# Twelve of the twenty modulation vectors of a two-block transformer kernel are finished one step later in the order of the engines

## The reference, cut to what matters

```python
c_act  = silu(c);  cc_act = silu(c_ctx)
mod_l = (c_act @ ada_w[i] + ada_b[i])[:, None, :]      # ada_w[i]: 1024 x 6144
mod_c = cc_act @ ada_w[i] + ada_b[i]
sh_a, sc_a, g_a, sh_m, sc_m, g_m = split(mod_l, 6)
h_l = modulate(rms_norm(x, norm_mix_g[i]), sh_a, sc_a)
...
x = x + g_a * y_l
x = x + g_m * mlp(modulate(rms_norm(x, norm_mlp_g[i]), sh_m, sc_m))
```

## Time and profile before

| what | value |
|---|---|
| time, median of 3 runs | 2417.89 us (2416.68 to 2421.29) |
| profiled execution, its own time | 2426.14 us |
| profiled execution, span of its instructions | 2424.2 us |
| granted TensorE clock, mean | 0.994 |
| TensorE busy with matmuls | 2386.3 us, 98% of the span |
| VectorE busy | 1610.2 us, 66% |
| ScalarE busy | 1192.7 us, 49% |
| GpSimd busy | 331.6 us, 14% |

### The profile page before, as it was taken

The page is one execution under the profiler, slowest core; times in us unless marked ns, Lnnn a source line. Parts: engine busy times, 40 slices in busy tenths (PEclk is TensorE's granted clock), DMA queues, the critical chain, the costliest instruction groups (busy, mean ns, idle before and its releaser), DMA issues.

```text
span 2424.2 us, 40267 instructions
## 1 busy us (share of the span) xinstructions
PE 2386.3 (98%) x17001; PEld 2189.1 (90%) x17001; DVE 1610.2 (66%) x2428; ACT 1192.7 (49%) x1977; POOL 331.6 (14%) x362
## 2 busy tenths in 40 slices
PE   8999999999999999999999999999999999999998
PEld 7999889999999998999997758878889888889998
DVE  5676676887777677678866865765653655466753
ACT  5445665544444567655554642421333444455643
POOL 1311002232132100035330001000001000001000
PEclk9999999999999999999999989999999999999999
DMA  7768634676676783466763211345542433334552
GB/s 238 228 224 221 201 109 135 219 237 208 217 241 224 208 224 121 123 200 223 244 200 108 55 46 53 122 166 182 189 158 87 150 104 105 120 117 146 179 195 96
DMA packets 374113, 401.54 MB, mean 166 GB/s; under 512 B 44708, under 2 KB 346048, under 8 KB 373677
## 3 DMA queue, kind: packets, MB, share of 16 engines
q1 hardware_dynamic: 371160, 391.19, 51.3%
q10 hardware_dynamic: 2772, 7.78, 1.0%
HBM read 397.87 MB, written 4.22 MB: 166 GB/s over the span
## 4 chain that ended last, share of the span: by engine, by line
PE 82%; DVE 11%; ACT 3%; issue 1%; POOL 1%; SPq 1%; DMA 0%; DVEq 0%; ACTq 0%; POOLq 0%
PE bank L685 25%; PE bank L687 24%; PE bank L686 24%; DVE rounded L2479 4%; PE bank L693 3%; DVE plain L2454 2%; ACT rounded L1670 2%; PE bank L698 1%; PE bank L1109 1%; PE bank L1139 1%; DVE plain L2464 0%; DVE plain L2712 0%; DVE plain L2752 0%; PE bank L1310 0%; ACT plain L2073 0%
## 5 line engine op out<-in xcount | busy, mean ns | idle before, releaser
L685 PE MATMUL bank<-rounded 128*128 128x256 f32 (+2 forms) x3480 | 1079.5, 310 | 7.5 <-DVE rounded L2479 2.9
L686 PE MATMUL bank<-rounded 128*128 128x256 f32 (+2 forms) x3480 | 1065.3, 306 | 0.0
L687 PE MATMUL bank<-rounded 128*128 128x256 f32 (+2 forms) x3480 | 1065.2, 306 | 0.0
L2479 DVE TENSOR_TENSOR rounded<-plain,rounded 128x1024 fp32r<-128x1024 f32 (+1 forms) x630 | 737.0, 1217 | 409.1 <-ACT rounded L1670 408.9
L1670 ACT ACTIVATE rounded<-plain 128x1024 fp32r<-128x1024 f32 (+1 forms) x630 | 616.4, 1032 | 359.1 <-PE bank L687 267.7
L685 PEld LDWEIGHTS bank<-rounded 128*128 128x128 f32 x3480 | 665.3, 191 | 53.5 <-issue 9.6
L687 PEld LDWEIGHTS bank<-rounded 128*128 128x128 f32 x3480 | 665.4, 191 | 29.0
L686 PEld LDWEIGHTS bank<-rounded 128*128 128x128 f32 x3480 | 665.7, 191 | 28.0
L685 PE MATMUL bank<-rounded,rounded 128*128 128x256 f32 (+2 forms) x1472 | 449.0, 305 | 5.7 <-DVE rounded L2479 2.3
L687 PE MATMUL bank<-rounded,rounded 128*128 128x256 f32 (+2 forms) x1472 | 445.4, 303 | 0.0
L686 PE MATMUL bank<-rounded,rounded 128*128 128x256 f32 (+2 forms) x1472 | 445.4, 303 | 0.0
(11 more groups left out here) (313 smaller groups left out, 1861.1 us busy)
## 6 DMA issues: line engine op xcount, KB each, us to landing
plain<-in_mlp_w SPq DMA_DIRECT2D x64, 1024.0 KB, 5.3
plain<-in_ada_w SPq DMA_DIRECT2D x48, 1024.0 KB, 5.5
plain<-in_ffn_w_gate SPq DMA_DIRECT2D x44, 1024.0 KB, 5.7
plain<-in_ffn_w_up SPq DMA_DIRECT2D x44, 1024.0 KB, 5.5
plain<-in_ffn_w_down SPq DMA_DIRECT2D x32, 1024.0 KB, 5.6
plain<-in_w_in SPq DMA_DIRECT2D x32, 1024.0 KB, 5.4
plain<-in_od_w_in SPq DMA_DIRECT2D x32, 1024.0 KB, 5.4
plain<-in_ffn_w_down SPq DMA_DIRECT2D x16, 768.0 KB, 6.3
```

The costliest lines, as they stand in the source:

```text
L685: pe.matmul(dst, a[0], b[0], start=first and i == 0, stop=False)
L686: pe.matmul(dst, a[0], b[1], start=False, stop=False)
L687: ins = pe.matmul(dst, a[1], b[0], start=False, stop=last and i == n - 1)
L2479: dve.tensor_tensor(low, raw, top, SUB).then_inc(*done(("lo", m, half)))
```

## The change

The step of vector 0 of each piece becomes the one after the step of its fourth `ada_w` unit. Vector 1 stays where it was: `step + 1 + 1` is the old `step + 2`, and `step + 1 + 2` the old `step + 3`. So 12 of the 20 vectors move by one step, and 8 don't.

```diff
@@ -103,7 +103,7 @@
     for (s, step), u in ADA_AT.items():
         if u % 4 == 3:
             for v in CHUNKS[u // 4][2]:
-                out[s, step + (3 if step == 26 else 2) * v] = (u // 4, v)
+                out[s, step + 1 + (2 if step == 26 else 1) * v] = (u // 4, v)
     return out
```

## The result

| | kernel before | changed kernel |
|---|---|---|
| median | 2419.05 us (22 runs, 2416.68 to 2424.94) | 2424.3 us (22 runs, 2418.34 to 2429.04 but for one) |
| ratio | | 1.0018, 95% interval 1.0011 to 1.0024 |
| profiled execution: its time, span | 2426.14, 2424.2 us | 2420.28, 2418.4 us |

The changed kernel is slower by some 4.4 us (2.7 to 5.8 by the interval). I had forecast 1.6 us and a time of 2419.5 us, at most 2423.0. One run of the changed kernel, at a mean clock of 0.751 and 2877.21 us, is left out of the ratio. The trace of the changed kernel is at the same time 5.8 us *shorter* than that of the kernel before. So a single pair of traces can't be subtracted as a whole; it has to be read place by place.

A forecast was written before the change was run, and what follows sets the result against it. TensorE, busy 98% of the span, was taken to bound the kernel. Twelve places paying 0.27 us less six saving it made 1.6 us, VectorE, banks and transfers 0: 2417.89 + 1.6 = 2419.5 us, range 2416.0 to 2423.0 us.

The forecast's parts named there:

- What bounds the kernel, and the two kinds of place: TensorE, busy 98%, bounds; at six of twelve old places it waits for VectorE's low half (4.52 us together), at six not.
- The term of the sum: On TensorE, twelve new places each pay 0.27 us and six old ones without a wait save it: 1.6 us longer.
- The larger sum that the prediction also gives and turns down: Starts of line 799's eight matmuls at least 25 ns apart: 0.11 us more per place, 2.3 us in all.
- VectorE, banks, transfers at nothing: Moved bias additions on VectorE, the ring of banks, fold buffers and `ada_w` transfers delay nothing: cost 0.
- step 12 of p0, where I expected a wait of some tenths: VectorE's line 2611 waits a few tenths of a microsecond for its products, only at this place; cost 0.
- The range and the chances: Whole kernel: 2416.0 to 2423.0 us; chances 0.05 slower by over 0.2%, 0.02 faster, 0.93 within 0.2%.
- rival 3: At step 5 of p0, idle time grown to 1.65 us halves the clock: 1.7 or 6.8 us more; chance 0.05.

The follow-up runs named there:

- e8: The changed kernel with the two folds of each piece put behind VectorE's next low halves instead of ahead of them; ratio to the kernel before 0.9992 (0.9983 to 1.0001).
- e2: Half of the change: against the kernel before, only the seven vectors of stages a0, b0, a1 and b1 move; ratio 1.0004 (0.9993 to 1.0015), median 2422.27 us.
- e3: The other half of the change: against the kernel before, only the five vectors of p0 move; ratio 1.0001 (0.9988 to 1.0014).
- e6: The kernel before with one vector alone moved, that of a1 at step 26; ratio 1.0002 (0.9994 to 1.0011).
- e1: The changed kernel once more, unaltered, against the kernel before; ratio 1.0017 (1.0004 to 1.0029), median 2425.03 us.
- e4: The kernel before with nothing moved, but three unread products (about 1.35 us) added as a delay at step 29 of a0; ratio 1.0008 (0.9998 to 1.0019).
- e5: Control: the kernel before, word for word, against itself; ratio 1.0006 (0.9998 to 1.0015).
- e7: The kernel before with vector 1 put at the old step of vector 0 instead of two or three steps later; ratio 1.0002 (0.9993 to 1.0010).
- e9: The kernel before with seven unread products keeping TensorE busy ahead of two waits of the convolution stage; ratio 0.9988 (0.9979 to 0.9997).
- e10: The changed kernel with seven unread products keeping TensorE busy ahead of two waits of the convolution stage; mean 2419.02 us (12 runs).
- e11: The changed kernel with both the later folds of e8 and the unread products of e10; median 2412.40 us, ratio to the kernel before 0.9964 (0.9950 to 0.9978).

## Why the prediction was wrong

**What bounds the kernel, and the two kinds of place:** right. Six of the twelve places had a wait in front, VectorE's row of multiply-adds and folds ahead of the low halves is what it is for (e8 takes it away and the waits go), and the waits grew by 0.18 us without the products.

**The term of the sum:** right in kind, and mis-sized: this is the first step that failed. "I take 0.27 us for each" stopped at the first matmul behind the products. The second is late by a further 0.10 us with 256 columns. By the lags of e2 and e3 a place costs 0.37 us five times and 0.41 us once: 5 x 0.37 + 0.41 = 2.3 us in place of 6 x 0.27 = 1.6 us. The row for it (the second matmul behind the products) is the one behind the last that I had read. The larger sum that the prediction also gives and turns down is 2.3 us as well, but by luck: it puts the missing time between the starts of the eight small matmuls, and these still lie within 0.06 us of each other (0.25 us for all, 0.19 for one).

**VectorE, banks, transfers at nothing:** right where it can be seen. Line 2611 has no idle time before it at any of the twenty places in the first trace of the change. At b0 it starts at 525.77 us, 4.5 us behind its products. At step 12 of p0, where I expected a wait of some tenths, it starts at 1654.57 us directly behind two low halves:

```profile
1652.29 2.36 DVE L2479 TENSOR_TENSOR rounded<-plain,rounded 128x1024 fp32r<-128x1024 f32 x2 [1.58 <-ACT rounded L1670]
1654.57 0.16 DVE L2611 TENSOR_TENSOR plain<-bank,plain 128x8 f32<-128x8 f32 x1
1659.80 0.88 DVE L2560 SCALAR_TENSOR_TENSOR plain<-bank,plain 128x256 f32<-128x256 f32 x2 [5.07 <-PE bank L687]
```

It arrives 0.7 us behind the products of 1653.84 us, and the idle time falls to the wait of line 2560 behind it, as reasoned.

**The range and the chances:** the second step that failed, and the larger one. I set them from the three runs shown, "its three runs lie 4.6 us apart", and took the rest of the kernel as fixed. It isn't: 93 later runs of the kernel before reach from 2416.36 to 2428.2 us, and the lower the mean clock of a run, the longer it is (correlation -0.80). The sign of it was on the table: the profiled execution was 8.3 us above the median. The reason stands in the earlier trace rows, and I used them for rival 3, which put the fall of the clock at step 5 of p0. There the wait of 1.65 us left the clock at 1.00 in every trace, as the work ahead of it had let me expect; the falls are where they were before, but for one at 797 us in e6.

**What is left.** Fixed cost 2.3 us, measured 4.35 (2.7 to 5.8) and in e1 4.1 us (1.0 to 7.0). The record can part the two, since it has the mean granted clock of every run. A stretch at half clock loses half of its length, so a run of 2420 us has lost about 2420 x (1 - mean clock) in all. This is an estimate: not all of that time is work that would have gone twice as fast (the 3.4 us of e6 cost 1.5 us and not 1.7), and the clock is on record in steps of 0.001, or 2.4 us. Here is the mean of each kernel against the kernel before beside it, as timed, then with this loss taken off every run, and by the lag of its one trace (without the shift at 260 us). Behind each is half of the 95% interval, from the spread of the runs:

| run | as timed, us | without the clock, us | by the lag, us |
|---|---|---|---|
| e1 | +3.6, 2.5 | +2.8, 1.5 | +2.6 |
| e2 | +1.1, 1.8 | +2.9, 1.3 | +2.2 |
| e3 | +0.5, 2.4 | +1.1, 1.6 | +0.4 |
| e4 | +1.4, 2.0 | +0.4, 1.2 | +1.0 |
| e5 (before) | +1.1, 1.7 | -1.2, 1.7 | +0.1 |
| e7 | 0.0, 1.9 | -3.3, 1.1 | -2.5 |
| e8 | -1.2, 1.8 | -4.6, 1.1 | -4.1 |
| e9 | -3.5, 1.8 | +0.5, 1.2 | -0.3 |
| e10 | -1.9, 1.6 | +2.5, 1.4 | +2.2 |
| e11 | -8.9, 1.4 | -4.4, 1.8 | -4.0 |

In all ten rows the difference without the clock agrees, within its interval, with what the lag says, and the gain of e9 is nothing but clock. In e6, which is not in the table, it does not agree (-0.9, 1.8 against 2.7 us by the lag), but the lag of its one trace holds the late transfer and 1.5 us of low clock. The 33 runs of the changed kernel are 2.6 us (1.8 to 3.3) above the 93 of before when the clock is taken off, and 2.8 us if 0.001 of clock is put at 1.8 us, as a straight line through the 93 runs has it. So outside the clock no more is seen than the fixed cost, with what the wait at 797 us may add.

The clock itself: the mean is 0.9952 in the 33 runs and 0.9956 in the 93, which makes 0.8 us, with 1.3 us to either side. That the change lowers it is not shown. The kernel before, set against itself in e5, has 0.9950 beside 0.9959, and e4 has 0.9949, no higher than the 0.9954 and 0.9950 of the two sets of runs of the changed kernel. In the first comparison part of the difference may also lie with the other side: its 22 runs of the kernel before have a mean of 2419.4 us, the 93 later ones, perhaps on other chips, 2420.9 us, and the clocks of the 22 are not on record. Against it speaks how many runs are high: 21 of the 33 with the change are at 2423 us or above, 20 of the 93 of before. A shift of 2.3 us by itself would carry 38 of the 93 over that line, 41%, and it is 64%. So the 2.3 us are shown; whether the other 2 us of the first comparison are chance, or falls of the clock that the change makes likelier, by the shift in time or by the wait at 797 us, stays open.

## What to carry to other kernels

Small work in front of a wait is free and becomes a cost where there is none, so move it towards the waits and not away from them. When pricing an interruption of a stream of matmuls, count up to the point where the usual pitch is back, not to the first matmul that follows. Before giving a range, ask why the profiled execution lies off the median; a state that changes from run to run can be larger than the edit, and then two traces are to be compared between points where that state is the same, or the state is to be steadied first, or what it cost each run is to be taken off its time.

## What the runs showed of the hardware that I had not expected

- The clock fell to 0.50 behind waits of 1.7 and 2.1 us in a stage of small products and stayed there for 3.4 or for 13.6 us while TensorE was busy throughout (13.60 of 13.60 us in e1), with the same code; behind the same wait of 1.74 us it did not fall in the first trace of the change, and in e2 it fell behind neither. Behind a wait of 1.65 us between dense matmuls it stayed at 1.00 in four traces. At 797 us, also between dense matmuls, it stayed at 1.00 behind a wait of 2.12 us and fell to 0.50 for 3.4 us behind one of 1.92 us (e6). The length of a wait alone does not tell whether the clock falls.
- Seven products that nobody reads, in those two waits, made the kernel before faster: 0.9988 (0.9979 to 0.9997), 2416.92 against 2419.83 us in the median.
- Eight small matmuls of line 799 start within about 0.06 us, sixteen within 0.13, but the stream of large ones around them loses 0.37 us for the first set and 0.06 us for a second right behind it.
- One transfer of 1 MB, issued at the same point with the same neighbour, took from 5.16 to 7.43 us in fourteen traces, and where the chain behind it had no slack the wait for it went from 0.64 to 2.12 us.
